# Expert weights loaded in pieces of 1 MB with runs of 8 KB per partition instead of 2 MB with 16 KB

## What is computed

```python
def clamped_swiglu_expert(xb, w_gu, b_gu, w_down, b_down):
    gu = xb @ w_gu + b_gu
    gate = jnp.minimum(gu[:, :D_FF], SWIGLU_LIMIT)
    up = jnp.clip(gu[:, D_FF:], -SWIGLU_LIMIT, SWIGLU_LIMIT)
    act = (up + 1.0) * (gate * jax.nn.sigmoid(gate * SWIGLU_ALPHA))
    return act @ w_down + b_down
...
  h = h + moe_ffn(rms_norm(h, norm_ffn_w), router_w, router_b, w_gu, b_gu, w_down, b_down)
```

## Time and profile before

| | us |
|---|---|
| median of 3 runs (lowest, highest) | 1324.82 (1324.72, 1338.38) |
| the profiled execution, its own time | 1326.72 |
| its span | 1324.8 |
| TensorE matmuls busy | 1188.7 (90%) |
| VectorE, GpSimd, ScalarE busy | 530.7, 276.4, 215.2 |
| matmuls of gate-up (line 1099) | 600.3 |
| matmuls of down (line 1114) | 295.2 |

### The profile page before, as it was taken

How to read it: one execution, slowest core, us unless ns; L and a number is a source line. 1 busy time by engine, 2 the same in 40 slices (tenths; PEclk the granted TensorE clock), 3 DMA queues, 4 the chain that set the end, 5 groups by cost and what they waited for, 6 DMA issues and landing times.

```text
span 1324.8 us, 30781 instructions
## 1 busy us (share of the span) xinstructions
PE 1188.7 (90%) x12045; PEld 551.5 (42%) x12046; DVE 530.7 (40%) x1333; ACT 215.2 (16%) x450; POOL 276.4 (21%) x372
## 2 busy tenths in 40 slices
PE   7999999998899889889888889899998987988895
PEld 6875556855333333333233333333333332333332
DVE  2337856557333333333333333343343332333332
ACT  3136664321100000000000000000000000000000
POOL 1000012000122222222222222232221221222222
PEclk9999999999999999999999999999999987999998
DMA  5132145088899999999999999999999999999994
GB/s 189 51 106 64 32 127 146 21 350 348 361 413 416 418 418 417 418 418 415 416 419 416 382 373 405 390 396 405 402 417 417 418 421 420 416 417 420 418 417 168
DMA packets 67649, 446.43 MB, mean 337 GB/s; under 512 B 16992, under 2 KB 37672, under 8 KB 43040
## 3 DMA queue, kind: packets, MB, share of 16 engines
q1 hardware_dynamic: 48736, 424.97, 77.6%
q0 software_dynamic: 16128, 18.78, 6.2%
q10 hardware_dynamic: 2752, 2.23, 0.5%
HBM read 435.24 MB, written 15.07 MB: 340 GB/s over the span
## 4 chain that ended last, share of the span: by engine, by line
DMA 62%; PE 23%; issue 6%; ACT 4%; DVE 3%; POOLq 1%; ACTq 0%; POOL 0%; SPq 0%; DVEq 0%
DMA out<-Y,IDXS 55%; PE PS L690 16%; DMA W<-in_expert_w_gate_up 4%; ACT Y L679 3%; PE PS L1099 3%; DMA XG<-hn_scratch,IDXC 2%; PE PSC L690 2%; PE PS L1114 1%; POOLq L443 0%; DMA W<-in_norm_mix_w 0%; PE PS L866 0%; PE PS L700 0%; DVE W L1165 0%; DVE W L1338 0%; DVE W L1337 0%
## 5 line engine op out<-in xcount | busy, mean ns | idle before, releaser
L1099 PE MATMUL PS<-W,XT 128*32 128x512 f32 x5184 | 600.3, 615 | 108.5 <-DVE XT L1517 90.3
L1099 PEld LDWEIGHTS PS<-W,XT 128*32 128x32 f32 x5184 | 167.8, 112 | 498.3 <-issue 405.2
L1114 PE MATMUL PS<-W,AT 128*32 128x256 f32 x5184 | 295.2, 379 | 2.7 <-DVE SIG L1545 2.2
L690 PE MATMUL PS<-W 128*128 128x512 f32 (+6 forms) x874 | 244.2, 437 | 2.1 <-ACT W L618 1.1
L1114 PEld LDWEIGHTS PS<-W,AT 128*32 128x32 f32 x5184 | 171.1, 110 | 146.9 <-issue 48.5
L1522 DVE TENSOR_TENSOR GU<-PS,BGU 128x512 f32<-128x512 f32 x81 | 56.0, 691 | 362.6 <-PE PS L1099 362.6
L690 PEld LDWEIGHTS PS<-W 128*128 128x128 f32 (+1 forms) x874 | 145.4, 190 | 81.9 <-issue 71.4
L679 ACT ACTIVATE Y<-SIG,ident 128x256 f32<-128x256 f32 x81 | 41.2, 508 | 812.3 <-DMA out<-Y,IDXS 801.4
L434 POOL DMA_INDIRECT out<-Y,IDXS x81 | 130.5, 1611 | 102.8 <-ACT Y L679 95.9
L1517 DVE STREAM_TRANSPOSE XT<-XG 128x256 f32<-128x256 f32 x81 | 52.0, 642 | 189.3 <-DMA XG<-hn_scratch,IDXC 189.3
L430 POOL COPY IDXS<-IDX 128x1 uint32 (+1 forms) x81 | 15.0, 185 | 493.1 <-DMA out<-Y,IDXS 493.1
(11 more groups left out here) (281 smaller groups left out, 523.7 us busy)
## 6 DMA issues: line engine op xcount, KB each, us to landing
W<-in_expert_w_gate_up SPq DMA_DIRECT2D x128, 2048.0 KB, 24.2
W<-in_expert_w_down SPq DMA_DIRECT2D x64, 2048.0 KB, 24.8
W<-in_w_in SPq DMA_DIRECT2D x10, 1024.0 KB, 5.5
W<-in_x SPq DMA_DIRECT2D x8, 512.0 KB, 11.1
W<-in_w_out SPq DMA_DIRECT2D x2, 1024.0 KB, 9.8
W<-in_w_out SPq DMA_DIRECT2D x1, 2048.0 KB, 8.0
hn_scratch<-W POOLq DMA_DIRECT2D x4, 512.0 KB, 11.9
out<-W ACTq DMA_DIRECT2D x4, 512.0 KB, 11.5
```

What stands on the lines that cost most here:

```text
L690: return pe.matmul(o, l, r, start=st, stop=sp_)
L1099: last = pe.matmul(GPS[32 * j:32 * j + 32, :].rearrange("p (g n) -> p g n", g=2), XT[:, 32 * k:32 * k + 32], rhs, start=(k == 0), stop=(k ...
L1114: last = pe.matmul(DPS[32 * j:32 * j + 32, :], AT[:, 32 * k:32 * k + 32], DNW[p][:, k, j * QW:(j + 1) * QW], start=(k == 0), stop=(k == KD ...
```

## The change

Each call that loaded a piece of two steps k (gate-up) or four (down) is replaced by two calls with half the steps each. The bytes, their places, their order and the waits ahead of the first half stay. A piece is now 1 MB with 8 KB for each partition. Both halves add 16 to the same semaphore, and TensorE waits for twice the value.

```diff
--- before.py
+++ after.py
@@ -220,14 +220,16 @@
                 for q in parts:
                     if through is not None:
                         sp.wait_ge(S_(f"gu_read{q}" if q < 3 else "gu_ps"), through)
-                    sp.dma_start(GUW[p][:, 2 * q:2 * q + 2, :],
-                                 w_gu[e].rearrange("(p k) n -> p k n", p=P)[:, 2 * q:2 * q + 2, :]).then_inc(S_(f"gu_in{p}{q}"), 16)
+                    for k in (2 * q, 2 * q + 1):
+                        sp.dma_start(GUW[p][:, k, :],
+                                     w_gu[e].rearrange("(p k) n -> p k n", p=P)[:, k, :]).then_inc(S_(f"gu_in{p}{q}"), 16)
             def dn_part(e, p, parts, through=None):
                 for q in parts:
                     if through is not None:
                         sp.wait_ge(S_("dn_read"), through) if q == 0 else sp.wait_ge(S_("d_ps"), through + 1)
-                    sp.dma_start(DNW[p][:, 4 * q:4 * q + 4, :],
-                                 w_dn[e].rearrange("(p k) n -> p k n", p=P)[:, 4 * q:4 * q + 4, :]).then_inc(S_(f"dn_in{p}{q}"), 16)
+                    for k in (4 * q, 4 * q + 2):
+                        sp.dma_start(DNW[p][:, k:k + 2, :],
+                                     w_dn[e].rearrange("(p k) n -> p k n", p=P)[:, k:k + 2, :]).then_inc(S_(f"dn_in{p}{q}"), 16)
             def small_parameters():
                 sp.dma_start(KWT, rep(kn_w)).then_inc(S_("par_in"), 16)
                 sp.dma_start(SIG[:, 0:64], rep(qn_w)).then_inc(S_("par_in"), 16)
@@ -1093,7 +1095,7 @@
                     pe.wait_ge(S_("gu_evac"), i)
                 for k in range(KD):
                     if first_of_expert and k % 2 == 0:
-                        pe.wait_ge(S_(f"gu_in{p}{k // 2}"), rnd)
+                        pe.wait_ge(S_(f"gu_in{p}{k // 2}"), rnd * 2)
                     for j in range(4):
                         rhs = GUW[p][:, k, :].rearrange("p (g n) -> p g n", g=2)[:, :, j * QW:(j + 1) * QW]
                         last = pe.matmul(GPS[32 * j:32 * j + 32, :].rearrange("p (g n) -> p g n", g=2),
@@ -1106,10 +1108,10 @@
             def down(i, p, rnd):
                 pe.wait_ge(S_("at_ready"), i + 1)
                 pe.wait_ge(S_("y_ready"), i + 1)
-                pe.wait_ge(S_(f"dn_in{p}0"), rnd)
+                pe.wait_ge(S_(f"dn_in{p}0"), rnd * 2)
                 for k in range(KD):
                     if k == KD // 2:
-                        pe.wait_ge(S_(f"dn_in{p}1"), rnd)
+                        pe.wait_ge(S_(f"dn_in{p}1"), rnd * 2)
                     for j in range(4):
                         last = pe.matmul(DPS[32 * j:32 * j + 32, :],
                                          AT[:, 32 * k:32 * k + 32],
```

## The result

The changed kernel takes 1333.28 us (median of 20 runs, 1329.39 to 1334.61), the kernel before 1326.14 beside it: ratio 1.0049 with an interval of 1.0036 to 1.0062. That is slower by 0.5%, 4.8 to 8.2 us. The forecast was 1323.0, 0.1% quicker: the range held the time, the sign was wrong. The profiled execution took 1332.75 us, its span 1331.0, against 1326.72 and 1324.8: +6.2 us in the span.

The account below looks back on a forecast made before the run. Total bytes on full DMA engines were taken as the floor, with blocks paced by packets queuing behind weights. Packets +7.8, closings +1.3, gaps -9.4 and the end -1.5 gave -1.8 us: 1323.0 from 1324.8, range 1313 to 1336.

Parts of the forecast that it names:

- Twice the packets, same bytes: Weight queue q1: as many packets again, of half the size, for the same bytes; 1440 more per engine.
- Shorter turns: Gathers and scatters among weight packets: scatter 2.7 us shorter, blocks paced by TensorE's 10.5 us instead of 12.2.
- I take 5.4: Full DMA engines: each added weight packet costs 5.4 ns, +7.8 us in all, ends 0 and +13.0.
- I take all of the 9.4 back: Stretch 740 to 980 us: shorter turns win back all the engines' empty time, -9.4 us, ends 0 and -9.4.
- The end, -1.5: After the last weights: an earlier second-last scatter lets the last one finish sooner, -1.5 us, ends 0 and -3.
- More issues on SP, 0: SP's queue of loads: 192 more issues, 64 us of SP, covered by pieces standing in line; 0, at most +1 us.
- the slower one (1339): Rival, full stretches: each added packet costs the recorded 9 ns and the gaps of 740 to 980 stay, 1339 us; chance 0.12.
- Every transfer paying by itself: Rival, weight loads: each transfer has a fixed part of some 1.8 us that nothing hides, +324, 1649 us; chance 0.01.
- Turns not shortened: Rival, DMA queues: weights get two short packets in a row, scatters stay, only the price remains, 1334 us; chance 0.14, shared with gaps kept.
- The quicker stream: Rival, weight stream: half as long turns win back 1.5% of 960 us, 14 us, giving 1309 us; chance 0.09.

Follow-up runs that it names:

- The dose with 4 KB runs: Weights in 1 MB pieces as in the changed kernel, but in runs of 4 KB instead of 8 KB: 1360.61 us, ratio 1.0272 to the kernel before.
- the stages alone: Separate kernel without computation, loading 24 MB of weights per stage: 61.2 us with 16 KB runs in 2 MB pieces, 62.0 with 8 KB in 1 MB, 64.7 with 4 KB.
- Gaps filled with a third of the packets: Kernel before with 1 MB pieces and 8 KB runs only for experts 12 to 21, 16 KB elsewhere: 1327.02 us, ratio 1.0012.
- spread slots: Tokens in a block reordered so its empty slots no longer stand together at the end: changed kernel 1321.90 us, kernel before 1317.55.
- The best version: Kernel before with the new order of token slots and only the down matrix in 8 KB runs: 1313.67 us, ratio 0.9912 to the kernel before.
- the spread kernel before: Kernel before with only the order of tokens in a block's slots changed, weights still in 16 KB runs: 1317.55 us, ratio 0.9949.

## Why the prediction was right or wrong

*Twice the packets, same bytes:* right. *Shorter turns:* right in mechanism and size. I had the scatter 2.7 us shorter and it is 2.1, blocks at 10.5 to 10.8 and they are at 10.3, TensorE's new wait near 100 us and it is 96 (from 59 blocks; 7412 matmuls are 58), the gaps of the middle gone. A new one at 1171 to 1178 I didn't have (7 x 0.31/1.02 = 2.1 us).

*"I take 5.4":* wrong, and the first of the two steps that failed. I took off the overlap of the recorded durations because the engine is full; but in a stream of long packets the share stayed at 1.02 when they were halved, so the recorded difference is what was paid. In the clean stretches 417 or 418 GB/s became 412 or 413, 1.2%, which is 11.8 us over some 970, closings included, against 9.1 in my sum. The dose with 4 KB runs gives 9.5 to 10.3 ns a packet, the recorded lengths 627 - 618 = 9 to 10 ns, the stages alone 7 to 13. So the term is 12 to 14 us. The section "Why small descriptors are slow" of "DMA: Bandwidth & Descriptors" in the Trainium skill, from which I had an estimate of 3.5 ns, names a second cost beside its 3 cycles, descriptor metadata moved with every operation; the runs show the sum of whatever there is, 8 to 10 ns at 8 KB, more than twice that estimate.

*"I take all of the 9.4 back":* wrong, and the larger failure. The rows were right, and the mean engine got its 9.4 us (240 x 16/410). But a DMA share is a mean over sixteen engines, and a piece of weights is there only when the last of them has brought its part. The fullest engine carries the same weights as the others and more of the scattered rows; in the gaps it had nothing to move for only some 5 us, by the landings above, and caught up in the rest. Its end, the last weights, moved by +8.0: 11.8 to 14.3 paid, so 4 to 6 back. Gaps filled with a third of the packets gave 3 back. With spread slots only 240 x 0.01/1.02 = 2.4 us of gaps are left, and 11.8 - 2.4 = 9.4 stands against a measured shift of the last weights of 8.7. There the mean comes close, though not exactly: by GB/s (417, 408 and 419 against 412, 411 and 414, to 1290) the same bytes cost 4.9 - 1.8 + 3.7 = 6.8 us, and the engines of the kernel after still end further apart than those before, 11.7 against 3.7 us. That the engine furthest behind sets the end is shown by the landings and by the spread runs; that it is behind for its scattered and gathered rows is borne out by the spread runs, but which engine moves which row isn't recorded, and the engines drift apart with spread slots too, only less.

*The end, -1.5:* right; what follows the last weights is 1.8 us shorter (2.4 with spread slots).

*More issues on SP, 0:* SP does wait in its own issues, which I had put under what would make me wrong. The engines stay at 1.02 meanwhile, so nothing shows that it costs time; a run that frees SP was not made, and this stays open.

*The clock*, which I had not named: TensorE's granted clock fell from 0.976 to 0.959 in the profiled executions. Nothing makes it the cause: with spread slots the changed kernel has 0.958 and is 0.73% quicker, and TensorE waits for weights.

Corrected with what was measured apart from the result: 11.8 to 14.3 paid, 3.2 back for the gaps (the kernel with short runs in the middle alone; 0.6 to 5.9 by its interval), 1.8 at the end: +7 to +9 us, the measured +6.5 by ratio and +6.2 in the spans lying within the interval of the middle term.

The rivals: the slower one (1339) had the price right and the gaps wrong. Every transfer paying by itself falls with the stages of 1 and 2 MB pieces and by its own size, 1649. Turns not shortened falls with the 8.6 us scatter; its 1334 is near the measured time by chance, from a smaller price and no return. The quicker stream falls with 412 GB/s. The best version beats the spread kernel before by 0.37% (0.9912 against 0.9949, 3.9 us by medians) although it pays some 4.7 us for its packets. That is more than 2.4 us of gaps and the end would give back; where the rest comes from stays open.

## What to carry to other kernels

Where DMA engines are full, price every packet that a finer cut adds at what the records of the two lengths differ by, here 8 to 10 ns, undiscounted; the number of transfers cost nothing here with several in flight. Read the floor at the engine furthest behind, not at the mean share: if a stream fades over 10 us instead of stopping, or the sixteen landings of one piece lie that far apart, engines are unequal, and gaps in the mean are worth less than they look. Spreading the padded rows over the partitions brought more here than any cut of the stream. Shorter runs buy shorter waits for what shares the engines; use them on as few bytes as fill the gaps.

## What the runs showed that I had not expected

- Transfers into 64 partitions moved 221 GB/s with all engines at 1.02, against 412 for 128 partitions: a factor of 1.65 on the whole kernel from an innocent-looking split. A scatter beside it took 17.9 us.
- An issue on SP stands still while the queue is full, and full is counted in packets rather than bytes: 16.4 us against 33.5 for the same 24 MB in the same 12 issues. A chain that says "SP 36%" can mean a saturated stream.
- The order of empty slots inside a block was worth 0.5% before and 0.7% after, more than the change under study.
